# Attention in a two-layer decoder: what the score matmuls wait for, where copies of probabilities stand, how retention blocks share banks, and how the final norm is applied

## The reference, cut to what matters

```python
for l in range(DEPTH):                                   # DEPTH = 2
    x = x + 0.5 * g1 * swiglu(h, ffn1_w_up[l], ffn1_w_down[l])
    x = x + g2 * hybrid_mixer(h, ...)                    # the stage that changes
    x = x + 0.5 * g3 * swiglu(h, ffn2_w_up[l], ffn2_w_down[l])
return rmsnorm(x, final_norm)                            # the end that changes

# sliding-window attention: 16 query heads of 64, blocks of 128 tokens, each sees its own and the previous block
m = jnp.max(logits, axis=-1, keepdims=True)              # logits: masked scores and one sink
p = jnp.exp(logits - m)
probs = p[..., :-1] / jnp.sum(p, axis=-1, keepdims=True)
out = jnp.einsum('bkgnij,bnjkd->bnikgd', probs, v2)

# retention: 4 heads, keys of 128, values of 256, computed here over all 512 tokens
scores = (q @ k.T) * decay                               # causal, decay[i, j] = gamma ** (i - j)
ret = scores @ v
```

## Time and profile before

| | us |
|---|---|
| median of 3 runs | 2602.13 (2601.56 to 2603.2) |
| profiled execution, its own time | 2599.23 |
| profiled execution, span of the trace | 2597.4 |
| PE busy | 2502.4 (96% of the span) |
| DVE busy | 1537.0 (59%) |
| ACT busy | 869.8 (33%) |
| mixer rounds in layer 0, in layer 1 | 508 to 737, 1763 to 1992 |
| end of the kernel after the last projection | 2577 to 2597 |

### The profile page before, as it was taken

One profiled execution on the slowest core, in us unless ns is written; L12 is line 12 of the kernel. 1 busy time (PEld: TensorE's weight loads), 2 busy tenths in 40 slices (PEclk: granted clock), 3 DMA queues, 4 the chain that ended last, 5 costly groups with the idle time before them and its releaser, 6 DMA issues.

```text
span 2597.4 us, 35934 instructions
## 1 busy us (share of the span) xinstructions
PE 2502.4 (96%) x11581; PEld 2045.3 (79%) x11581; DVE 1537.0 (59%) x2345; ACT 869.8 (33%) x1320; POOL 212.9 (8%) x167
## 2 busy tenths in 40 slices
PE   5999999999999999999999999999999999999998
PEld 4788888777678878888878888887777888788886
DVE  6876778566644467633477767866665445633333
ACT  2331233545422243222332222344543223331222
POOL 5100003000000040000030000210000002200001
PEclk7999999999999999999999999999999999999999
DMA  6465664311123425523336656532111343233332
GB/s 222 125 199 166 194 183 132 122 56 50 57 68 96 129 88 170 159 85 96 110 91 194 188 177 195 160 122 60 54 57 49 99 128 97 85 100 95 95 111 66
DMA packets 494952, 307.19 MB, mean 118 GB/s; under 512 B 8904, under 2 KB 488472, under 8 KB 494232
## 3 DMA queue, kind: packets, MB, share of 16 engines
q1 hardware_dynamic: 427288, 239.10, 31.1%
q10 hardware_dynamic: 67584, 67.12, 8.1%
HBM read 299.89 MB, written 6.29 MB: 118 GB/s over the span
## 4 chain that ended last, share of the span: by engine, by line
PE 76%; DVE 13%; ACT 5%; issue 4%; POOL 1%; DVEq 0%; DMA 0%; ACTq 0%; SPq 0%; POOLq 0%
PE ps_proj L1468 23%; PE ps_proj L1469 23%; PE ps_proj L1470 23%; ACT sb_scratch L680 2%; DVE sb_w_lo L871 2%; DVE sb_small L1142 2%; DVE sb_scratch L1139 1%; PE ps_mid L1624 1%; PE ps_mid L1626 1%; PE ps_mid L1625 1%; DVE sb_scratch L1162 1%; PE ps_mid L1672 1%; POOL sb_scratch L461 1%; DVE sb_h_lo L938 1%; DVE sb_scratch L883 1%
## 5 line engine op out<-in xcount | busy, mean ns | idle before, releaser
L1468 PE MATMUL ps_proj<-sb_a_hi,sb_w_hi 128*128 128x512 f32 x1888 | 736.1, 390 | 3.0 <-DVE sb_w_lo L871 3.0
L1470 PE MATMUL ps_proj<-sb_a_hi,sb_w_lo 128*128 128x512 f32 x1888 | 734.7, 389 | 0.0
L1469 PE MATMUL ps_proj<-sb_a_lo,sb_w_hi 128*128 128x512 f32 x1888 | 734.5, 389 | 0.0
L533 ACT ACTIVATE sb_w_hi<-sb_raw 128x1024 fp32r<-128x1024 f32 (+1 forms) x388 | 431.0, 1111 | 872.6 <-PE ps_proj L1470 833.2
L871 DVE TENSOR_TENSOR sb_w_lo<-sb_raw,sb_w_hi 128x1024 fp32r<-128x1024 f32 (+1 forms) x388 | 503.4, 1297 | 310.9 <-ACT sb_w_hi L533 295.5
L1468 PE MATMUL ps_proj<-sb_h_hi,sb_w_hi 128*128 128x512 f32 x1280 | 511.9, 400 | 10.7 <-DVE sb_w_lo L871 6.3
L1469 PE MATMUL ps_proj<-sb_h_lo,sb_w_hi 128*128 128x512 f32 x1280 | 502.7, 393 | 0.0
L1470 PE MATMUL ps_proj<-sb_h_hi,sb_w_lo 128*128 128x512 f32 x1280 | 502.2, 392 | 0.0
L1468 PEld LDWEIGHTS ps_proj<-sb_a_hi,sb_w_hi 128*128 128x128 f32 x1888 | 354.4, 188 | 79.4 <-issue 3.0
L1470 PEld LDWEIGHTS ps_proj<-sb_a_hi,sb_w_lo 128*128 128x128 f32 x1888 | 354.4, 188 | 73.3
L1469 PEld LDWEIGHTS ps_proj<-sb_a_lo,sb_w_hi 128*128 128x128 f32 x1888 | 354.4, 188 | 73.0
(11 more groups left out here) (162 smaller groups left out, 1863.4 us busy)
## 6 DMA issues: line engine op xcount, KB each, us to landing
sb_raw<-in_ffn_w_up SPq DMA_DIRECT2D x176, 512.0 KB, 3.8
sb_scratch<-in_w_ada ACTq DMA_DIRECT2D x128, 512.0 KB, 4.2
sb_raw<-in_w_in SPq DMA_DIRECT2D x100, 512.0 KB, 3.8
sb_raw<-in_ffn_w_down SPq DMA_DIRECT2D x64, 704.0 KB, 4.5
sb_raw<-in_w_branch_swa SPq DMA_DIRECT2D x16, 512.0 KB, 3.6
sb_raw<-in_w_branch_ret SPq DMA_DIRECT2D x16, 512.0 KB, 3.6
sb_raw<-in_w_out SPq DMA_DIRECT2D x16, 512.0 KB, 3.6
sb_scratch<-in_w_ada SPq DMA_DIRECT2D x14, 512.0 KB, 7.4
```

The lines of the kernel that those rows point to most:

```text
L533: act.activation(Whi[s][:, 0:n], raw[s][:, 0:n], ACT.Copy).then_inc(hi_ready, 1)
L1468: pe.matmul(bank, Whi[s][:, w], hi, start=first, stop=False)
L1469: pe.matmul(bank, Whi[s][:, w], lo, start=False, stop=False)
L1470: return pe.matmul(bank, Wlo[s][:, w], hi, start=False, stop=last)
```

## The change

Six things are done.

1. A semaphore `masked` is signalled by the mask-add of `maxima`, and PE's score matmuls wait for it instead of `max_ready`. `exps` still waits for `max_ready`.
2. On DVE `probs_out(h0)` and `probs_out(h0+1)` stand ahead of `normalise` of the next call; on ACT they stand ahead of `exps` of the next call.
3. The first `maxima` of a head moves to the end of the loop body of the head before, and for head 0 between the two query halves.
4. Retention blocks 1 (384 columns) and 3 (128 columns) share bank 1: both score matmuls are issued together, one signal covers both, and the values of block 2 come last. There are three parts instead of four.
5. In the last layer ACT multiplies each finished tile of x with the gain (`final_scale`). PE transposes the first four tiles ahead of the sum of squares, the others behind it, and DVE and ACT apply the reciprocal root, now a scalar per row, while they copy from PSUM.
6. The output is stored in four transfers of 128 tokens each, 512 KB, instead of two.

```diff
+RET_BLOCKS = ((0,), (1, 3), (2,))
+RET_AT = {0: (0, 0), 1: (1, 0), 3: (1, T - P), 2: (0, 0)}
...
 # scalar (ACT)
                     exps(h0, 0)
                     swap(b + 1, 0, g + 1, rope0 + 2, pA[0], P // 2)
                     split_weights(b + 2, 0, UP_UNIT)
+                    probs_out(h0)
                     exps(h0 + 1, 1)
                     swap(b + 1, 1, g + 1, rope0 + 3, pA[1], P // 2)
                     split_weights(b + 2, 1, UP_UNIT)
-                    probs_out(h0)
+                    probs_out(h0 + 1)
                     exps(h0 + 2, 0)
...
-                            probs_out(h0 + 1)
                             exps(h0 + 3, 1)
...
+            act.wait_ge(rstd_ready, 4 * DEPTH + 1)
+            for n in range(TT):
+                act.wait_ge(y_last, n + 1)
+                act.activation(out_tok[:, n, T:2 * T], last_banks[n][:, :], ACT.Copy, scale=rstd[:, n:n + 1]).then_inc(o_last, 1)
...
 # vector (DVE)
-                st.mark(dve.tensor_tensor(probs[w].rearrange("p (a t) -> p a t", a=2), pM[:, 0:2, :],
-                                          mask.unsqueeze(1).broadcast_to([P, 2, T]), ALU.add))
-                st.wait()
+                dve.tensor_tensor(probs[w].rearrange("p (a t) -> p a t", a=2), pM[:, 0:2, :],
+                                  mask.unsqueeze(1).broadcast_to([P, 2, T]), ALU.add).then_inc(masked, 1)
+                dve.wait_ge(masked, no + 1)
...
-                    maxima(h0, l, i, 0, 0, 0)
                     retention_rope(0, rq)
                     normalise(h0, 0)
                     maxima(h0 + 1, l, i, 0, 1, 1)
+                    probs_out(h0)
                     normalise(h0 + 1, 1)
                     retention_rope(1, rk)
-                    probs_out(h0)
                     maxima(h0 + 2, l, i, 1, 0, 0)
+                    probs_out(h0 + 1)
                     normalise(h0 + 2, 0)
                     retention_gate(0)
-                    probs_out(h0 + 1)
                     maxima(h0 + 3, l, i, 1, 1, 1)
...
+                with st.loop(0, RH - 1, 4 + 4 * 4) as i:
                     middle(i)
                     tail(i, True)
+                    first_maxima(i + 1)
...
+                dve.tensor_scalar(out_tok[:, n, 0:T], pM[:, n, :], rstd[:, n:n + 1], None, ALU.mult).then_inc(o_first, 1)
...
 # tensor (PE)
-                    pe.wait_ge(max_ready, h0 + 1)
+                    pe.wait_ge(masked, h0 + 1)
...
                     ret_values(0)
                     ret_scores(2)
                     ret_values(1)
-                    ret_scores(3)
-                    ret_values(2)
-                    ret_values(3).then_inc(y_ps, 1)
+                    ret_values(2).then_inc(y_ps, 1)
```

More of the change, by code:

```diff
@@ L314, in in_next_layer, with in_last_layer @@
                     work()
+        def in_last_layer(eng, l, work):
+            with eng.If(l > DEPTH - 2):
+                work()
         def next_layer(l):
@@ L423, in _ @@
                 ffn_loads(l, 1, 1)
[L424 to L429, removed]
+            for n in range(TT):
+                sp.wait_ge(o_first, n + 1)
+                sp.wait_ge(o_last, n + 1)
+                sp.dma_start(out[0].rearrange("(t p) d -> p t d", p=P)[:, n, :], out_tok[:, n, :]).then_inc(stored, 16)
+            sp.wait_ge(stored, 16 * TT)
         @block.gpsimd
@@ L557, in load_next_layers_job, with final_scale @@
                         act.dma_start(ada_raw[s], ada_v[next_l, n, s]).then_inc(ada_in[s], 16)
+            def final_scale(k):
+                act.activation(XV[:, k, :], XV[:, k, :], ACT.Copy, scale=vcols[:, bass.ds(GAIN_COL["final"] + k, 1)]).then_inc(z_ready, 1)
             def scaled_hi(no, k):
@@ L1316, in tail, with decay @@
                     h0 = 4 * n0
-                    def decay(n):
-                        w = T - P * n
-                        dve.wait_ge(st_ps, TT * n0 + n + 1)
-                        dve.tensor_tensor(ret_s[n % 2][:, 0:w], pM[:, n % 2, 0:w], K[:, bass.ds(K_DECAY + T * i, w)],
-                                          ALU.mult).then_inc(st_done, 1)
+                    def decay(part):
+                        dve.wait_ge(st_ps, RET_PARTS * n0 + part + 1)
+                        for n in RET_BLOCKS[part]:
+                            w, (bank, at) = T - P * n, RET_AT[n]
+                            last = dve.tensor_tensor(ret_s[bank][:, at:at + w], pM[:, bank, at:at + w], K[:, bass.ds(K_DECAY + T * i, w)], ALU.mult)
+                        last.then_inc(st_done, 1)
                     swa_out(2 * n0, 2 * i)
@@ L1342, in tail, with first_maxima @@
                         dve.tensor_tensor(XV[:, 2 * i + e, :], pM[:, 2 + e, :], silu_g[:, e, :], ALU.mult).then_inc(y_free, 1)
-                for s in range(2):
-                    start_query(0, s)
-                    split_weights(b + 2, s, UP_UNIT)
-                with st.loop(0, RH - 1, 4 + 4 * 5) as i:
+                def first_maxima(i):
+                    maxima(4 * numbers(i)[3], l, i, 0, 0, 0)
+                start_query(0, 0)
+                split_weights(b + 2, 0, UP_UNIT)
+                first_maxima(0)
+                start_query(0, 1)
+                split_weights(b + 2, 1, UP_UNIT)
+                with st.loop(0, RH - 1, 4 + 4 * 4) as i:
                     middle(i)
                     tail(i, True)
+                    first_maxima(i + 1)
                 middle(RH - 1)
```

72 lines of the change are left out of this document (43 added, 29 removed).

## The result

| | before | after |
|---|---|---|
| median | 2601.85 us (2599.65 to 2603.2, 4 runs) | 2575.61 us (2574.76 to 2577.58, 4 runs) |
| ratio, 95% interval | | 0.9901 [0.9887, 0.9914] |
| span of the profiled execution | 2597.4 us | 2572.9 us |
| its own time | 2599.23 us | 2574.76 us |

The changed kernel is 26 us faster; 2575.9 had been forecast. That alone doesn't show that the reasons were right. The trace of the changed kernel says which of the steps came true; I read it in the order of the prediction.

The account below looks back on a forecast made before the run. The prediction took a closed loop through DVE and ACT in each head, not PE, as the bound. Two mixers at 20.6 us plus the end at 5.6 gave 26.2; 2602.1 - 26.2 = 2575.9 us, range 2568 to 2590.

Parts of the forecast that it names:

- The loop: Each head is a closed loop through DVE and ACT, 57.60 us before; PE's gaps in it are slack.
- Scores wait for the masked copy: PE's scores in heads 1 to 3: gain nothing; idle time moves to the values, about 1.5 us there.
- Copies ahead of normalise: Two DVE copies of 0.60 us move into idle time in the loop's first part: 1.20 us per head, 8 heads.
- Two retention blocks per bank: Loop's third part, last retention values: 0.5 us gained in heads 0 to 2, 0.1 in head 3.
- First maxima early: Start of head 0: exponentials start 3.9 us earlier; other heads gain nothing.
- The mixer's sum: Gains of the four heads, 5.6 + 1.7 + 1.7 + 1.3 = 10.3 us per layer, 20.6 for two.
- The end: Final norm and stores: first store at 2584.2, 7.6 us of transfers, end at 2591.8, a gain of 5.6 us.
- that rival: Stores at the end do not overlap: four transfers in a row at 3.8 us each, 2583.8 us; chance 0.06.
- the prediction's 12.8 us: Output stores at the end: four separate transfers by the skill's fixed 2.0 us plus bytes at 436 GB/s.
- PE as the bound: Rival: PE's waits go and nothing replaces them, middle heads gain 3.77 us each, 2557.7 us; chance 0.05.
- the rival's mechanism: Clock falls after idleness gathered before the values: 1.6 us lost per head, 12.8 in all, 2588.7 us; chance 0.09.
- The moved copies: Rival: copies waiting for PE's transposes delay exponentials and normalise; 33 us lost at 5 us late, 2608.9 us; chance 0.04.

Follow-up runs that it names:

- both ways of the first item: Scores waiting for the maxima again in the changed kernel, 2575.79 us; scores waiting for the masked copy as the only edit to the kernel before, 2602.55 us.
- unneeded work on PE: Changed kernel plus eight unneeded transposes per head on PE, just ahead of the third call's values: 2575.76 us.
- another order on DVE and ACT: Changed kernel with attention output and third call's copy of probabilities earlier on DVE and ACT, 2561.41 us; with block 2's decay earlier on DVE too, 2559.49 us.
- the fastest kernel: Changed kernel with attention output, third call's copy of probabilities and block 2's decay earlier: 2559.49 us; with scores waiting for the maxima again, 2573.16 us.
- the run with the unneeded transposes: Changed kernel with retention in four parts again, plus eight unneeded transposes per head on PE ahead of the third call's values: 2580.54 us.
- the first experiment: Changed kernel with only PE's score matmuls waiting for the maxima again: 2575.79 us.
- four parts: Changed kernel with retention in four parts again, block 3's scores between the values of blocks 1 and 2 and its values last: 2590.11 us.
- the copies back: Changed kernel with copies of probabilities back behind the rope and the gate on DVE and behind the exponentials on ACT: 2586.92 us.
- the first item alone: Kernel before with only one edit, PE's score matmuls waiting for the masked copy: 2602.55 us, ratio 1.0007.

## Why the prediction was right, step by step

**The loop.** Right, though PE is part of it in its second part, and carried by five runs: both ways of the first item (nothing), unneeded work on PE (nothing), and another order on DVE and ACT (14 and 16 us). The three parts of the loop, forecast 39.76, 13.07 and 3.07 us, measured 39.90 (566.52 to 606.42), 13.05 (to 619.47) and 3.12 (to 622.59).

**Scores wait for the masked copy.** Costed at nothing, worth nothing. The idle time moved to the values, 1.67 us where "about 1.5" had been written. What the prediction did not say is that the item is needed for the next step: 13.7 us in the fastest kernel.

**Copies ahead of normalise.** 1.20 us per head forecast, 57.27 - 56.07 = 1.20 measured.

**Two retention blocks per bank.** 0.5 forecast for heads 0 to 2, 0.48 measured by the run with the unneeded transposes; for head 3 0.1 forecast, 0.6 measured (50.89 less 50.31). That is 3.9 us in eight heads. Undoing the item alone cost 14.5, since the clock then fell in six heads. In the changed kernel the item therefore also keeps the clock, which the prediction did not see.

**First maxima early.** 3.9 forecast, 3.73 and 3.95 measured in the two layers. Head 0 was forecast at 55.6 us and takes 55.92 (508.55 to 564.47 from first scores to first scores).

**The mixer's sum** was somewhat too large: 10.3 us per layer forecast. Measured from the first scores to the projection behind the mixer, 228.38 us (508.22 to 736.60) less 218.37 (508.55 to 726.92), it is 10.0, and the same in layer 1. Head 0 gives 5.3 (61.22 less 55.92) where 5.6 was forecast, heads 1 and 2 1.53 each (57.60 less 56.07) where it was 1.7, most of this the 0.14 us by which the loop's first part is longer than forecast. Head 3 gives 1.66 (51.97 less 50.31) where it was 1.3.

Up to the end's first instruction the profiled executions differ by 2577.32 - 2559.17 = 18.15 us, where 20.6 was forecast and the two mixers give 20.05. The rest lies outside the change. The changed kernel's execution began its mixer 0.33 us later (508.55 against 508.22), and it lost 1.35 us in the norm at the start of layer 1, whose code is the same in both. There the granted clock fell behind 2.69 us of idleness, while in the kernel before it held behind 2.81. First the kernel before, then the changed one, each from the spreading of the root to the same projection:

```profile
1334.81:1358.53 23.72, 23.45 (x108) 19.28 (x108) 20.36 (x30) 11.79 (x17) 0.46 (x1) 1.00 0.38 112
```

```profile
1325.30:1350.37 25.07, 24.79 (x109) 20.52 (x109) 20.37 (x30) 11.82 (x17) 0.45 (x1) 0.94 0.35 106
```

**The end.** 5.6 forecast, 20.1 - 13.7 = 6.4 measured. Since item 5 was not undone alone, this is read from the two traces: the first store comes 6.8 us after the last projection, forecast 6.9, instead of 12.5, and that is 5.7 of the 6.4. What was mis-sized are the transfers: 2565.95 to 2572.9 are 6.95 us, where 7.6 was taken over from the kernel before. Those 7.6 us held a wait: the second store was issued only at 2592.85, 3.0 us after the first, when its last copies were done (2591.57 + 1.26), and the slice of 146 GB/s stands there. The full slices of the changed kernel hold 382 to 428 GB/s, the others of the kernel before 369 to 405. The four stores flow into each other, so that rival fell: it needed 15.5 us. Their number is not what made them faster, since two stores with the same rows of 1024 features also took 7.0 us; whether the rows, which had 512 features before, raise the rate was not tested alone. The Trainium skill, "DMA: Bandwidth & Descriptors", section Bandwidth, advises batches of at least 1 MiB; with two stores of 1024 KB the rate didn't rise (364 to 428 GB/s) and the end came 0.7 us later, for the batch has to be filled first. The fit behind the prediction's 12.8 us stands on that page of the Trainium skill in the section "Anatomy of one DMA", not under Bandwidth, and for transfers issued by GpSimd; these are issued by SyncE.

Taken together the mixers gave 20.05 us of 20.6 and the end 6.4 of 5.6, two errors that nearly cancel. The spans differ by 24.5 us, 1.7 less than forecast, and the medians by 26.2, as forecast. The step between the two is no larger than the spread of the runs of one kernel, so that 2575.6 lies so near 2575.9 is in part luck.

**The rivals.** PE as the bound fell with the first experiment. The clock did not fall in the mixers of this kernel, but the rival's mechanism is real. Its price of 1.6 us per head is right for the middle heads; with four parts the last head lost 2.8 and head 0 nothing, 11.9 us in all where the rival had 12.8. The chance given to it, 0.09, was argued from one gap that kept the clock (1.55 us) and one that lost it (2.15). The gap came out at 1.67, and at 1.91 the clock was lost. How near 1.67 is to that the runs don't say: with the copies back, gaps of 1.81 and 1.85 kept it. The moved copies did not tie the exponentials to PE: DVE's wait ahead of normalise is 1.6 us with the copy in front of it, as forecast.

## What to carry to other kernels

Ask of each wait whether the loop that sets the period passes through it, by following one period from an instruction to its next occurrence on the engine that never has slack. Shortening a wait beside the loop only moves the idle time; in this kernel it was worth 0, and 13.7 us after the loop had been cut. And look at where the idle time moves to: pieces that are harmless one by one may gather ahead of one instruction.

## What the runs showed of the hardware

- In the mixers the granted clock fell behind single gaps of PE of 1.90 to 1.93 us (heads 1 to 3 with four parts), 2.15 (head 0 before), 2.43 and 3.20, in work that was otherwise dense, and did not behind 1.67 or less. The gap's length alone doesn't decide: 1.89 and 1.92 us in head 0 with four parts kept the clock, as did 1.81, 1.85 and 1.89 with the copies back; 1.85 in the last head with the first item alone kept it in layer 0 and lost it in layer 1 (1.00 and 0.97); at the norm of layer 1, 2.81 kept it in the kernel before and 2.69 lost it in the changed one. What else decides is open.
- A fall costs time only where PE's work sets the pace. Behind the gap ahead of the third call's values it cost 1.6 us in a middle head and 2.8 in the last; earlier in head 0 it cost nothing (57.13 us with the copies back, the forecast 1.2 more than 55.92); so did it in the last head with the first item alone (51.97 us at 1.00 and at 0.97). At the norm of layer 1 it cost 1.35 us.
- Unneeded work on an engine can make a kernel faster: eight transposes per head took 9.6 us off the kernel with four parts (2590.11 to 2580.54), and cost nothing in the changed one.
- Four stores of 512 KB from one queue, with rows of 1024 floats, ran without a dip at 382 to 428 GB/s, and two of 1024 KB with the same rows at 364 to 428.
